# Adding the residual to the output rows in memory by accumulating transfers, instead of on VectorE

## What is computed

```python
h = rmsnorm(x, p['g_pre2']) * (1 + sc2) + sh2
f = lax.map(lambda hs: moe_tokens(hs, p), h)      # 64 experts, top 8, plus one shared expert
x = x + gt2 * rmsnorm(f, p['g_post2'])            # the output rows
```

## Time and profile before

| | |
|---|---|
| median of three runs | 1247.88 us (1246.65 to 1248.0) |
| the profiled execution's own time | 1246.15 us |
| its span, first to last instruction | 1244.2 us |
| mean granted TensorE clock | 0.971 |
| busy over the span | PE 93%, DVE 45%, POOL 42%, ACT 26% |
| moved by DMA | 337.44 MB, mean 271 GB/s |

### The profile page before, as it was taken

One profiled execution on the slowest core, in us unless ns is written; L12 is line 12 of the kernel. 1 busy time (PEld: TensorE's weight loads), 2 busy tenths in 40 slices (PEclk: granted clock), 3 DMA queues, 4 the chain that ended last, 5 costly groups with the idle time before them and its releaser, 6 DMA issues.

```text
span 1244.2 us, 26196 instructions
## 1 busy us (share of the span) xinstructions
PE 1157.4 (93%) x9253; PEld 852.7 (69%) x9254; DVE 560.7 (45%) x912; ACT 327.3 (26%) x620; POOL 524.7 (42%) x527
## 2 busy tenths in 40 slices
PE   4899999999999899978899999978999997999897
PEld 3699999999999899966755555544455554555452
DVE  3285677659568868227743322211112221222134
ACT  3523322322333451335211221111111211111122
POOL 2144444445448244310665554452345444344420
PEclk9899999999999999998999999999999999999999
DMA  9954344424421232438789999999999999999987
GB/s 310 322 171 153 93 144 152 152 84 152 152 84 34 68 101 85 136 128 310 285 304 389 406 404 408 408 409 415 411 409 409 408 400 400 407 401 401 353 314 276
DMA packets 157224, 337.44 MB, mean 271 GB/s; under 512 B 14807, under 2 KB 99363, under 8 KB 139753
## 3 DMA queue, kind: packets, MB, share of 16 engines
q1 hardware_dynamic: 137496, 296.57, 64.2%
q0 software_dynamic: 16656, 34.14, 7.3%
q10 hardware_dynamic: 3025, 6.07, 1.4%
HBM read 322.21 MB, written 33.30 MB: 286 GB/s over the span
## 4 chain that ended last, share of the span: by engine, by line
PE 58%; SPq 20%; DMA 7%; issue 6%; DVE 6%; POOL 2%; ACT 1%; DVEq 0%; POOLq 0%; ACTq 0%
PE ps L1746 14%; SPq L356 12%; PE ps L1509 10%; PE ps L1510 9%; PE ps L1511 9%; PE ps L1760 6%; SPq L361 6%; DMA w<-in_w_dram 4%; DMA ring<-in_w_ada_dram 2%; PE ps L1522 1%; PE ps L1852 1%; SPq L388 1%; PE ps L1451 1%; PE ps L1754 1%; PE ps L1819 1%
## 5 line engine op out<-in xcount | busy, mean ns | idle before, releaser
L1746 PE MATMUL ps<-w,xe 128*64 x3136 | 367.2, 388 | 37.9 <-DMA w<-in_w_dram 32.1
L1746 PEld LDWEIGHTS ps<-w,xe 128*64 128x64 f32 x3136 | 229.6, 140 | 171.8 <-issue 77.5
L534 POOL TENSOR_TENSOR wsplit<-ring,wsplit 128x1024 fp32r<-128x1024 f32 x80 | 194.8, 2435 | 282.3 <-ACT wsplit L687 250.8
L1509 PE MATMUL ps<-h_s_hi,wsplit 128*128 128x260 f32 x960 | 272.4, 284 | 0.0
L1511 PE MATMUL ps<-h_s_hi,wsplit 128*128 128x260 f32 x960 | 270.8, 282 | 0.0
L1510 PE MATMUL ps<-h_lo_m_hi,wsplit 128*128 128x260 f32 x832 | 234.8, 282 | 0.0
L1371 DVE TENSOR_TENSOR rs<-sg,ps 128x128 f32<-128x128 f32 x98 | 28.2, 287 | 375.9 <-ACT sg L985 375.9
L1760 PE MATMUL ps<-w,eactT 128*64 (+1 forms) x784 | 185.2, 593 | 0.9 <-issue 0.8
L1509 PEld LDWEIGHTS ps<-h_s_hi,wsplit 128*128 128x128 f32 x960 | 180.6, 188 | 6.9 <-issue 5.9
L1511 PEld LDWEIGHTS ps<-h_s_hi,wsplit 128*128 128x128 f32 x960 | 180.8, 188 | 0.0
L687 ACT ACTIVATE wsplit<-ring 128x1024 fp32r<-128x1024 f32 x80 | 84.8, 1060 | 298.3 <-PE ps L1511 288.0
(11 more groups left out here) (333 smaller groups left out, 1344.1 us busy)
## 6 DMA issues: line engine op xcount, KB each, us to landing
w<-in_w_dram SPq DMA_DIRECT2D x192, 1024.0 KB, 20.8
ring<-in_w_in_dram SPq DMA_DIRECT2D x56, 512.0 KB, 3.7
ring<-in_w_ada_dram SPq DMA_DIRECT2D x8, 2048.0 KB, 8.7
ring<-in_w_ada_dram SPq DMA_DIRECT2D x8, 1024.0 KB, 21.9
ring<-y_rows SPq DMA_DIRECT2D x4, 2048.0 KB, 17.9
ring<-in_w_out_a_dram SPq DMA_DIRECT2D x8, 512.0 KB, 4.1
ring<-in_w_out_b_dram SPq DMA_DIRECT2D x8, 512.0 KB, 4.1
ring<-in_w_o_dram SPq DMA_DIRECT2D x8, 512.0 KB, 4.1
```

The source lines that it names most:

```text
L534: pool.tensor_tensor(wsplit[:, b, 1], raw[raw_slot], wsplit[:, b, 0], ALU.subtract).then_inc(S["w_lo"], 1)
L1509: mm(ps[:, bank + h, 0:HT], wsplit[:, b, 0, k, :], hi[:, k, p:q], start=(k == 0), stop=False)
L1746: ins = mm(ps[a * STRIP:(a + 1) * STRIP, 2 + f, 0:2 * P], xe[:, k, a * STRIP:(a + 1) * STRIP], w[a][:, k, :, f * P:(f + 1) * P], start=(k ...
```

## The change

The scratch tensor `x1_dram` goes. ScalarE's queue stores the five x1 tiles straight into the output tensors, at the same places in its stream. SyncE no longer loads x1 back, and VectorE no longer adds it. VectorE's product of L1408 is itself the tile that goes out: GpSimd's queue issues five transfers with `accum_op=add`, each of which adds a tile of 128 x 1024 (the last one 8 x 1024) to what the output tensor holds. Each tile has an output buffer of its own, two of them where x1 was kept. SyncE's five stores and its wait for them go; GpSimd waits for the five transfers instead. TensorE's wait ahead of the sample's shared expert now counts the same product by another name (`fin_out` in place of `yacc`).

```diff
-    x1_dram = nc.dram_tensor("x1_dram", (T, D), F32, kind="Internal").ap()
...
-        x1b = [slot_part(0, YF, D), slot_part(0, YF + D, D), slot_part(1, YF, D), slot_part(1, YF + D, D), slot_part(2, YF, D)]
...
-        outb = [hflat[:, D:2 * D], slot_part(4, YF, D), slot_part(4, YF + D, D)]
+        outb = [hflat[:, D:2 * D], slot_part(4, YF, D), slot_part(4, YF + D, D), slot_part(0, YF, D), slot_part(1, YF, D)]
...
+        def y_tile(i):
+            return y_prompt[0, i * P:(i + 1) * P, :] if i < TT - 1 else y_sample.rearrange("n a d -> (n a) d")
...
-            x1_back(0)
-            x1_back(1)
...
-            x1_back(2)
-            x1_back(3)
...
-            x1_back(TT - 1)
...
-            for n in range(TT):
-                i = order[n]
-                sp.wait_ge(S["fin_out"], n + 1)
-                dst = y_prompt[0, i * P:(i + 1) * P, :] if i < TT - 1 else y_sample.rearrange("n a d -> (n a) d")
-                sp.dma_start(dst, outb[n % 3][0:P if i < TT - 1 else LAST, :]).then_inc(tile_out[n % 3], 16)
-
             sp.wait_ge(out_done, 16 * 6)
-            for b in range(3):
-                sp.wait_ge(tile_out[b], 16 * (2 if b < TT - 3 else 1))
...
+            pool.wait_ge(spill, 16 * TT)
+            for n in range(TT):
+                i = order[n]
+                pool.wait_ge(S["fin_out"], n + 1)
+                pool.dma_start(y_tile(i), outb[n][0:P if i < TT - 1 else LAST, :], accum_op=ALU.add).then_inc(tile_out, 16)
+            pool.wait_ge(tile_out, 16 * TT)
...
-                act.dma_start(x1_dram[i * P:(i + 1) * P, :], x1tok[:, i, :]).then_inc(spill, 16)
+                act.dma_start(y_tile(i), x1tok[:, i, :]).then_inc(spill, 16)
...
-                buf, r = outb[n % 3][0:rows, :], nrm[0:rows, 1, n:n + 1]
+                buf, r = outb[n][0:rows, :], nrm[0:rows, 1, n:n + 1]
...
-                    dve.wait_ge(spill, 16 * TT * 2)
-                if n >= 3:
-                    dve.wait_ge(tile_out[n % 3], 16)
                 stt(out=buf, in0=ps[0:rows, f:f + 2, :].rearrange("p b n -> p (b n)"), scalar=r, in1=(G2 if i < TT - 1 else G2s)[0:rows, :],
-                    op0=ALU.mult, op1=ALU.mult).then_inc(S["yacc"], 1)
-                dve.wait_ge(S["yacc"], n + 1)
-                tt(buf, buf, x1b[i][0:rows, :], ALU.add).then_inc(S["fin_out"], 1)
+                    op0=ALU.mult, op1=ALU.mult).then_inc(S["fin_out"], 1)
...
-            pe.wait_ge(S["yacc"], 1)
+            pe.wait_ge(S["fin_out"], 1)
```

More of the change, by code:

```diff
@@ L275, in build_program @@
                  "ex_y ex_yd gcopy scopy passed yb_free es_dve es_pe "
-                 "yacc fin_sq root_act fin_out").split()
+                 "fin_sq root_act fin_out").split()
         S = {n: sem(n) for n in names}
@@ L283, in build_program @@
         order = tuple(range(TT))
-        tile_out = [sem(f"tile_out{b}") for b in range(3)]
+        tile_out = sem("tile_out")
         g2_out, g2_in = sem("g2_out"), sem("g2_in")
@@ L412, in slot_free @@
                 passed()
-            def x1_back(i):
-                n = P if i < TT - 1 else LAST
-                sp.dma_start(x1b[i][0:n, :], x1_dram[i * P:i * P + n, :]).then_inc(spill, 16)
             def tile_rows(dst, i, h, landed):
@@ L917, in _ @@
                 act.wait_ge(S["x1t_dve"], i - 1)
-                act.dma_start(x1_dram[i * P:i * P + n, :], x1tok[0:n, i, :]).then_inc(spill, 16)
+                act.dma_start(y_tile(i), x1tok[0:n, i, :]).then_inc(spill, 16)
             hx_at = [hx[:, 0, :], hx[:, 1, :], conv[:, 0:D], sflat[:, 0:D]]
```

## The result

The changed kernel takes **1252.61 us** in the median of six runs (1251.13 to 1254.63), the kernel before 1248.04 in as many (1246.65 to 1249.37). The ratio is 1.0044, 95% interval 1.0033 to 1.0054: slower by 0.4%, where no change was forecast, and above the range (1244.8 to 1251.8). In the profiles the span goes from 1244.2 to 1249.1 us.

The account below looks back on a forecast made before the run. TensorE bounds the kernel to about 1232.7 us, then ScalarE and VectorE to the last store; -2.15 (additions) + 1.6 (last transfers) = -0.55 us, so 1247.3 against a median of 1247.88, range 1244.8 to 1251.8.

Parts of the forecast that it names:

- VectorE's additions: At the kernel's end: five x1 additions of 1.2 us go, so the sample's product ends at 1239.65 instead of 1241.80, gaining 2.15 us.
- rival A: TensorE's wait ahead of tile 3's last half: accumulations of tiles 0 and 1 delay its y_last, about 4 us; chance 0.15.
- The loads back: SyncE's queue: without the five x1 loads, y_last landings come earlier, giving tile 3's about 3.1 us of slack before TensorE.
- the first accumulations: GpSimd's transfers of tiles 0 and 1 delay y_last of tile 3 from 1229.2 to 1231.9; slack covers it, cost zero.
- backlog of 5.1 us: Slow DMA engines take 5.1 us for 2 MB; without the loads, y_last of tile 0 lands at 1209.5 instead of 1214.6.
- adding might count twice: Accumulations of tiles 0 and 1: if reading the destination counts too, the loss cap is 5.2 us, held to 4.
- cap for both tiles charged once: Without slack, 1 MB of tiles 0 and 1 charged once delays y_last of tile 3 by at most about 2.6 us.
- The estimate by an even split: DMA engines alternating evenly between queues: y_last of tile 3 lands up to 5.2 us after 1229.2, TensorE about 2 late.
- The last transfers: At the end: GpSimd's accumulating sample transfer takes 3.5 us to land against 1.9 for SyncE's store, losing 1.6 us.
- Rival B: Last transfers: accumulation itself lands slowly, tile 3's taking 9.1 us and landing at 1247.1, for 1251.2 us; chance 0.11.
- its sign: What would show rival B: more than 5 us between VectorE's end and the end of the span.
- From the last landing to the end: End of the program: the last store lands at about 1243.7 and the span closes at 1244.2; GpSimd has only its own end.

## Why the prediction was wrong

The sum had two terms and came to -0.55 us. In the profiles it is +4.95, by these steps:

- **VectorE's additions, -2.15.** The mechanism and the size were right: -2.15 with the residual left out and SyncE's stores kept. What failed is that it stayed in the sum undiminished. 1.51 us went to rival A, so that -0.64 was left.
- **The loads back give 3.1 us of slack.** This step failed, and with it the term "cost zero" of the first accumulations. The prediction passed a backlog of 5.1 us on from tile to tile. In the runs it ends with tile 0: y_first of tile 3 landed at 1198.4 instead of 1207.5, y_last of tile 0 at 1211.5 instead of 1214.7, but y_last of tile 1, issued at 1210.87 once a scatter had landed and with 0.7 us of tile 0's left ahead of it, still took 9.0 us, where I had put some 7.5, and tile 3's gained 0.45 us.

  The sixteen steps by which a landing's semaphore is counted up, which stand in the trace of before and in none of its views, show how: the last three of y_first of tile 3 come at 1203.4, 1205.4 and 1207.5; of y_last of tile 0 fourteen are in by 1211.3 and two follow at 1214.0 and 1214.7; of tile 1's fifteen are in by 1219.7 and one comes at 1220.7. The late ones caught up by themselves from load to load, so that there was little left to gain for tile 3.

  That adding might count twice was right as a rate: 188 against 406 GB/s. Which of the two tiles took the time no run separates: tile 0's transfer is over at 1232.6, ahead of y_last of tile 3, and its 0.52 MB at 188 GB/s are 2.8 us of all engines; the prediction's cap for both tiles charged once was 2.6; that load lost 2.4. The estimate by an even split, 1234.4, is where the load landed, but by luck: it counts from 1229.2, while with the two transfers left out the load lands at 1232.0.
- **The last transfers, +1.6.** Measured +2.0. The nearest rows came close, 5.0 for tile 3 measured 5.1 and 3.5 for the sample 3.6, in part by luck: they hold no adding, and the plain transfers of this queue took 2.9 and 2.1. What was missing is 0.28 us between VectorE's end and GpSimd's issue. Rival B did not come true, though its sign did (7.8 us between VectorE's end and the end of the span, where more than 5 was to tell of it): the sign could not tell a slow landing from what comes behind the landing. The Trainium skill's formula ("DMA: Bandwidth & Descriptors", the section on the anatomy of one DMA), 2.1 and 3.2 us, fits the plain transfers of this queue, 2.1 and 2.9, and not the accumulating ones.
- **From the last landing to the end, 0.5 us as before.** This was taken over from SyncE without a thought, and it is the largest miss: +3.4 us for GpSimd's drain. "GpSimd has no work behind these waits; only its own end comes after them" was the sentence; its own end had a price, and it stood in the trace of before, 20 us ahead of the end, where nothing waited for it.

Together -0.64 + 2.0 + 3.4 is 4.8, and 0.17 us lie ahead of the stage. Rival A was named with the right place and mechanism and 0.15 as its chance; it came true at 1.5 us instead of 4. The drain was in no rival. Without it the change would, by these numbers, still have been some 1.5 us slower, where the sum had it 0.55 faster: within the 2.5 us that the forecast took as no change, but with the wrong sign.

What stays open: what the drain does in its 3.1 us, and why it is 5.2 with a transfer in flight, no run shows. The runs only show that behind landed transfers it goes with their number: 3.10 us with none of these transfers on GpSimd's queue, 3.34 with three, 3.51 with five, plain or adding, early or late. The remaining few tenths by which the expected and the measured ends differ were not pursued.

## What to carry to other kernels

When the last work of a program moves to another engine, look up what that engine does at the end of its stream: the trace of before showed it here, off the path and in none of the page's groups. In these runs the stores that stood behind the loads on SyncE's queue delayed y_last of tile 3 by under 0.4 us, and the same tiles on GpSimd's queue by 1.5 plain and 2.4 adding, so look whose landing is awaited at that moment and how much slack it has. And a backlog that was removed helped here only the landings up to the next transfer that was issued late for another reason.

## What the runs showed that I had not expected

GpSimd's drain at the end of its stream took 3.10 us in the kernel before, whether 20 us ahead of the end or last, 3.3 to 3.5 us behind transfers that had landed and 5.2 us, its last issue included, right behind an issue. A transfer that adds in memory kept all DMA engines busy at 188 GB/s, a plain one of the same tile on the same queue at 406. And the same 32 KB from GpSimd's queue took 2.1 us plain and 3.6 us adding.
